# Two-layer diffusion backbone on one core: products by stream of 256 columns, operands moved by 64 bytes, the latent half first at the joins of stages

## The reference

```
z = modulate(rmsnorm(h), m0, m1);  h += 0.5*m2 * ((silu(z@Wg) * (z@Wu)) @ Wdown)   # 2 x 2816 columns, back to 1024
z = modulate(rmsnorm(h), m3, m4);  p = z @ W_in_mix                                # x, gelu input, u, v: 4 x 512
   RG-LRU: conv of x, sigmoid gates by head, forward and backward scan, * gelu
   spatial gate: u * (w_s @ layernorm(v) + b_s)
h += m5 * (concat(y_lru, y_sgu) @ W_out_mix)
z = modulate(rmsnorm(h), m6, m7);  h += 0.5*m8 * swiglu(z)
```

## Time and profile before

| | |
|---|---|
| median of 3 runs | 1624.05 us (1623.73 to 1624.52) |
| the profiled execution | 1623.73 us |
| its span | 1621.9 us |
| PE busy | 1572.3 us, 97%, 8,804 matmuls |
| PE weight loads | 1317.5 us, 81%, 8,804 |
| DVE busy | 1030.4 us, 64% |
| ACT busy | 633.2 us, 39% |
| POOL busy | 109.3 us, 7% |
| TensorE clock, mean | 0.99 of full |
| HBM read | 247.62 MB, 153 GB/s |

### The profile page before, as it was taken

One profiled execution on the slowest core, in us unless ns is written; L12 is line 12 of the kernel. 1 busy time (PEld: TensorE's weight loads), 2 busy tenths in 40 slices (PEclk: granted clock), 3 DMA queues, 4 the chain that ended last, 5 costly groups with the idle time before them and its releaser, 6 DMA issues.

```text
span 1621.9 us, 24555 instructions
## 1 busy us (share of the span) xinstructions
PE 1572.3 (97%) x8804; PEld 1317.5 (81%) x8804; DVE 1030.4 (64%) x1498; ACT 633.2 (39%) x841; POOL 109.3 (7%) x117
## 2 busy tenths in 40 slices
PE   5999999999999999999999999999999999789998
PEld 4788888888778787788888888888888877789997
DVE  6777778233777467787742368777753368856554
ACT  4322222222663364334422242222222248467752
POOL 0000000011200300000000110000001030110001
PEclk9999999999999999999999999999999999999999
DMA  9455555343322335555533325555533323445563
GB/s 379 148 182 189 183 188 187 130 156 129 92 78 73 110 112 179 188 183 186 186 124 101 114 91 183 188 186 186 189 125 109 103 78 117 142 149 193 191 208 117
DMA packets 89047, 249.43 MB, mean 154 GB/s; under 512 B 13472, under 2 KB 14624, under 8 KB 87840
## 3 DMA queue, kind: packets, MB, share of 16 engines
q1 hardware_dynamic: 88992, 248.71, 47.0%
HBM read 247.62 MB, written 1.05 MB: 153 GB/s over the span
## 4 chain that ended last, share of the span: by engine, by line
PE 88%; DVE 5%; issue 2%; DMA 2%; ACT 1%; POOL 1%; DVEq 0%; SPq 0%; POOLq 0%; ACTq 0%
PE bank L361 27%; PE bank L362 27%; PE bank L363 27%; DMA ada_raw<-ada_w 2%; PE bank L612 1%; DVE ada_acc L1030 1%; PE bank L381 1%; DVE w_lo L851 1%; PE bank L594 1%; PE bank L592 1%; PE bank L593 1%; DMA res<-x_t 0%; PE bank L465 0%; PE bank L407 0%; POOL tokr L1302 0%
## 5 line engine op out<-in xcount | busy, mean ns | idle before, releaser
L851 DVE TENSOR_TENSOR w_lo<-raw,w_hi 128x1024 fp32r<-128x1024 f32 x320 | 391.5, 1225 | 416.2 <-ACT w_hi L677 249.9
L361 PE MATMUL bank<-z_hi,w_hi 128*128 128x512 f32 (+1 forms) x1574 | 575.7, 366 | 8.3 <-DVE v_n L1160 2.7
L362 PE MATMUL bank<-z_lo,w_hi 128*128 128x512 f32 (+1 forms) x1574 | 567.6, 361 | 0.0
L363 PE MATMUL bank<-z_hi,w_lo 128*128 128x512 f32 (+1 forms) x1574 | 567.0, 360 | 0.0
L683 ACT ACTIVATE w_hi<-raw 128x1024 fp32r<-128x1024 f32 x176 | 186.5, 1060 | 428.2 <-PE bank L363 427.4
L361 PEld LDWEIGHTS bank<-z_hi,w_hi 128*128 128x128 f32 x1574 | 296.3, 188 | 63.0 <-issue 10.0
L363 PEld LDWEIGHTS bank<-z_hi,w_lo 128*128 128x128 f32 x1574 | 296.2, 188 | 46.0
L362 PEld LDWEIGHTS bank<-z_lo,w_hi 128*128 128x128 f32 x1574 | 296.4, 188 | 45.7 <-issue 1.9
L1030 DVE SCALAR_TENSOR_TENSOR ada_acc<-ada_raw,c_cols,ada_acc 128x512 f32<-128x512 f32 x420 | 288.9, 747 | 8.0 <-DMA ada_raw<-ada_w 6.7
L677 ACT ACTIVATE w_hi<-raw 128x1024 fp32r<-128x1024 f32 x136 | 143.9, 1059 | 350.8 <-PE bank L363 344.5
L361 PE MATMUL bank<-h_hi,w_hi 128*128 128x512 f32 (+1 forms) x704 | 254.2, 361 | 0.1
(11 more groups left out here) (136 smaller groups left out, 1069.4 us busy)
## 6 DMA issues: line engine op xcount, KB each, us to landing
raw<-weights SPq DMA_DIRECT2D x320, 512.0 KB, 3.3
ada_raw<-ada_w SPq DMA_DIRECT2D x240, 256.0 KB, 3.0
ada_head<-head_w SPq DMA_DIRECT2D x8, 1024.0 KB, 20.3
ada_z<-ada_w SPq DMA_DIRECT2D x4, 1024.0 KB, 5.8
res<-x_t SPq DMA_DIRECT2D x1, 2048.0 KB, 8.0
bd<-gate_w SPq DMA_DIRECT2D x4, 256.0 KB, 5.3
out<-res SPq DMA_DIRECT2D x4, 256.0 KB, 2.2
ws<-sgu_w SPq DMA_DIRECT2D x2, 256.0 KB, 5.6
```

The source lines that it names most:

```text
L361: pe.matmul(bank_ap, w_hi[:, r, c], rhs_hi, start=start, stop=False, skip_group_check=True)
L362: pe.matmul(bank_ap, w_hi[:, r, c], rhs_lo, start=False, stop=False, skip_group_check=True)
L363: return pe.matmul(bank_ap, w_lo[:, r, c], rhs_hi, start=False, stop=stop, skip_group_check=True)
L851: dve.tensor_tensor(w_lo[:, r, :], raw[:, r, :], w_hi[:, r, :].bitcast(F32), ALU.subtract).then_inc(lo_ready, 1)
```

## The change

Products are made by stream: each of the three matmuls of a product is issued for columns 0 to 255 and for 256 to 511, with the same weight block. `LAT0` goes, every operand starts at column 0, and `row_pad` moves from ahead of h to ahead of `raw`, `w_hi` and `w_lo`, which moves these and all up to h by 64 bytes, while z, h and y stay. At the joins with two streams (norms 1 to 4) the last row of a down stage (the last two rows of the out stage of layer 0) is computed for the latent stream first; the sums and the spread of the latent half stand amid the context products. The first slots (three in mix too) run all blocks of the latent half, then all of the context half; the context half's sums and spread stand behind blocks 1 and 4. The gap units of norm 1 move ahead of the last row. All of z_lo goes to VectorE. The mix stage shifts by one slot (`GATE_LAG` 3), the spatial gates get four banks, slot 12 waits for all eight copies, and all of `y_hi` is made at slot 15.

```diff
-GATE_LAG = 2
-SIDE = 2
-UP_SIDE = 3
+GATE_LAG = 3
+SIDE = 3
-MIX_HI_DVE = range(6, 10)
+MIX_HI_DVE = range(7, 11)
-LAT0 = 112
         z_lo = sb("z_lo", [P, KD, T], F32R)
+        sb("row_pad", [P, 16])
         raw = sb("raw", [P, RING, SLOT])
...
-        sb("row_pad", [P, 16])
...
-        x_bank = pa[0:2] + po
+        x_bank = pa[0:3] + po[1:2]
+        ss_bank, spread_bank = (p_misc, po[0]), (po[1], p_misc)
...
+        def split_rows(n):
+            return () if n == 0 or streams(dft(n)) == 1 else (6, 7) if n % 3 == 2 else (7,)
...
+        def tail_bank(d, s, n):
+            return po[d % 2] if s == 0 or d not in split_rows(n) else pa[3] if d == KD - 1 else p_ada
...
-            def product(bank_ap, blk, r, rhs_hi, rhs_lo, start, stop):
+            def product(bank, blk, r, x_hi, x_lo, k, ss, start, stop):
                 c = slice(blk * P, (blk + 1) * P)
-                pe.matmul(bank_ap, w_hi[:, r, c], rhs_hi, start=start, stop=False, skip_group_check=True)
-                pe.matmul(bank_ap, w_hi[:, r, c], rhs_lo, start=False, stop=False, skip_group_check=True)
-                return pe.matmul(bank_ap, w_lo[:, r, c], rhs_hi, start=False, stop=stop, skip_group_check=True)
+                for i, (w, x) in enumerate(((w_hi, x_hi), (w_hi, x_lo), (w_lo, x_hi))):
+                    for s in ss:
+                        m = pe.matmul(bank[:, COLS[s]], w[:, r, c], x[:, k, COLS[s]], start=start and i == 0 and s == ss[0],
+                                      stop=stop and i == 2, skip_group_check=True)
+                return m
...
+                for s in ss:
+                    for k in range(KD):
+                        c = slice(k * P, (k + 1) * P)
+                        pe.wait_ge(z_hi_ready, z_piece(n, k, s))
+                        for q, dst in enumerate(banks):
+                            pe.matmul(dst[:, COLS[s]], w_hi[:, q, c], z_hi[:, k, COLS[s]], start=(k == 0 and s == 0),
+                                      stop=False, skip_group_check=True)
+                            pe.matmul(dst[:, COLS[s]], w_lo[:, q, c], z_hi[:, k, COLS[s]], start=False,
+                                      stop=False, skip_group_check=True)
+                        pe.wait_ge(z_ready, z_piece(n, k, s))
...
+                        if len(ss) == 2 and s == 0:
+                            if k == 1:
+                                norm_sums(n, 1)
+                            if k == 4:
+                                norm_spread(n, 1)
...
+                def row_by_stream(d):
+                    q = 3 * d
+                    pe.wait_ge(lo_ready, at["slot"] + q + 3)
+                    pe.wait_ge(res_ready, HID0 - 1 + at["tile"] + d)
+                    for s in ss:
+                        for k in range(8):
+                            m = product(tail_bank(d, s, n), k, q % RING, h_hi, h_lo, k, (s,), k == 0, False)
+                    m.then_inc(slot_done, 1)
+                    for s in ss:
+                        for k in range(8, KF):
+                            m = product(tail_bank(d, s, n), k % 8, (q + k // 8) % RING, h_hi, h_lo, k, (s,), False, k == KF - 1)
+                            if s == 0 and k == KF - 1:
+                                m.then_inc(lat_done, 1)
+                            if s == 1 and k in (15, KF - 1):
+                                m.then_inc(slot_done, 1)
+                            if s == 1 and k == 12:
+                                norm_sums(n, 0)
+                            if s == 1 and k == 18:
+                                norm_spread(n, 0)
...
+                    if AT["norm", n]["gap"]:
+                        for k in range(KD):
+                            gap_unit(n, k)
+                    row_by_stream(KD - 1)
...
                     if q == 12:
                         pe.wait_ge(vn_ready, l + 1)
+                        pe.wait_ge(copy_ready, 8 * (l + 1))
...
-                        dst = (p_ada, p_misc)[g % 2]
+                        dst = (p_ada, p_misc, po[0], po[1])[g]
...
+                def rows_by_stream():
+                    pe.wait_ge(lo_ready, at["slot"] + KD)
+                    for s in ss:
+                        for d in split_rows(n):
+                            if s == 0:
+                                pe.wait_ge(res_ready, HID0 - 1 + at["tile"] + d)
+                            for k in range(KD):
+                                m = product(tail_bank(d, s, n), k, d % RING, y_hi, y_lo, k, (s,), k == 0, k == KD - 1)
+                                if k == KD - 1:
+                                    m.then_inc(slot_done if s else lat_done, 1)
+                                if s == 1 and d == 6 and k == 4:
+                                    norm_sums(n, 0)
+                                if s == 1 and d == 7 and k == 1:
+                                    norm_spread(n, 0)
                 pe.wait_ge(copy_ready, 8 * (l + 1))
+                pe.wait_ge(zz_ready, 4 * (l + 1))
...
# ScalarE, mix stage
-                    for k in {14: (0, 1), 15: range(2, KD)}.get(q, ()):
+                    for k in range(KD) if q == 15 else ():
# ScalarE, norm
+                for d in split_rows(n):
+                    square_half(d, n, 0)
+                act.wait_ge(slot_done, base - 1)
+                split_hi(base + 2, 2)
+                if len(split_rows(n)) == 2:
+                    square_half(6, n, 1)
+                z_high(0, 0)
+                z_high(1, 0)
+                square_half(7, n, 1)
+                for k in range(2, KD):
+                    z_high(k, 0)
...
# VectorE, norm
+                for i, d in enumerate(split_rows(n)):
+                    dve.wait_ge(lat_done, split_before(n) + i + 1)
+                    residual(n, d, 0, res_lat_ready)
...
+                if split_rows(n):
+                    split_lo(base + 2, 2)
...
+                for s in range(streams(w)):
+                    scaled(0, s)
+                    for k in range(KD):
+                        if k + 1 < KD:
+                            scaled(k + 1, s)
+                        z_low(k, s)
+                        if split_rows(n) and s == 0 and k == 0:
+                            dve.wait_ge(slot_done, base)
+                            residual(n, KD - 1, 1, res_ready)
+                        if split_rows(n) and s == 0 and k == 3:
+                            variance(1)
+                        if split_rows(n) and s == 1 and k == 2:
+                            split_lo(base + 3, 3)
# VectorE, mix stage
-                    if q in (6, 7):
-                        scans(l, q - 6)
+                    if q in (7, 8):
+                        scans(l, q - 7)
...
+                    if q == 15:
                         y_low(l, 0, wl)
+                        spatial_gate(l, 3, wl)
                         y_low(l, 1, wl)
```

More of the change, by code:

```diff
@@ L506, in first_slots @@
[L506 to L511 removed]
+                for s in ss:
[8 more added lines that the diff above has]
+                        pe.wait_ge(z_ready, z_piece(n, k, s))
+                        for q, dst in enumerate(banks):
+                            m = pe.matmul(dst[:, COLS[s]], w_hi[:, q, c], z_lo[:, k, COLS[s]], start=False,
+                                          stop=(k == KD - 1 and s == ss[-1]), skip_group_check=True)
+                            if k == KD - 1 and s == ss[-1]:
+                                m.then_inc(slot_done, 1)
[4 more added lines that the diff above has]
+                                norm_spread(n, 1)
@@ L547, in down_stage @@
                 at = AT[l, "down", f]
[L548 to L564 removed]
+                n = 3 * l + 2 * f + 1
@@ new lines, in down_stage, with row @@
+                ss = range(streams(dft(n - 1)))
+                def row(d, dd):
+                    for part, n_blk in enumerate((8, 8, 6)):
+                        q = 3 * dd + part
+                        pe.wait_ge(lo_ready, at["slot"] + 1 + (d - dd) * 3 + q)
+                        if part == 0:
+                            pe.wait_ge(res_ready, HID0 - 1 + at["tile"] + d)
+                        for b in range(n_blk):
+                            k = 8 * part + b
+                            if dd == 0 and k in (0, KF - 2, KF - 1):
+                                pe.wait_ge(hid_lo_ready, HID_LO0 + at["ffn"] * KF + max(k + 1, KF - 2))
+                            m = product(po[dd % 2], b, q % RING, h_hi, h_lo, k, ss, k == 0, k == KF - 1)
+                        m.then_inc(slot_done, 1)
@@ L566, in in_stage @@
+                with pe.Fori(0, KD // 4 - (len(ss) == 2)) as i:
+                    for dd in range(4):
+                        row(i * 4 + dd, dd)
+                if len(ss) == 2:
+                    for d in range(4, KD - 1):
+                        row(d, d)
+                    if AT["norm", n]["gap"]:
+                        for k in range(KD):
+                            gap_unit(n, k)
+                    row_by_stream(KD - 1)
```

(22 more changed lines are left out.)

363 lines of the change are left out of this document (140 added, 223 removed).

## The result

The changed kernel takes 1643.84 us (median of 4 runs, 1640.48 to 1653.52) beside 1624.28 for the kernel before in the same session (1623.73 to 1624.76): ratio 1.013, 95% interval 1.0087 to 1.0173. Forecast were 1618.9 and a range up to 1627. The profiled execution took 1644.79, its span is 1642.8. The four runs of after lie 13 us apart, those of before 1 us.

A forecast was written before the change was run, and what follows sets the result against it. TensorE's chain of waits, 88% of the page's chain, was taken as the bound. From 1623.73 us, joins gave -11.7 and mix stages +1.5, +2.45 and +2.9, making 1618.9; the range was 1612 to 1627.

The forecast's parts named there:

- (a): Products of both streams: splitting each 512-column matmul into two of 256 costs 0; bounds 0 and 6.7 ns per half.
- rival B: Placement fails: one or both halves of a product run at 120 ns; 1653 or 1687 us, chance 0.12.
- the v slots: Slots streaming weights at +64 over z, 96 matmuls on layer 0's path: between -0.4 and +1.3 us, taken as 0.
- Rival C: Every matmul has a fixed price, paid once more per pair: 0.8 ns together, 4.1 us, 1623.0 us; chance 0.05.
- (b): Joins 3 and 4, last row by stream: 4.0 us left lost (3.1 to 5.5), gaining 2.7 and 4.2.
- (c): Join 2, mix to up, last two rows by stream: 4.3 us left lost (3.9 to 5.6), gaining 2.4.
- (d): Join 1, down to mix, with eight gap units now on the path: 8.1 us left (7.2 to 9.6), gaining 2.4.
- joins 1 to 4: Stage changes down to mix, mix to up, down to up, down to mix (layer 1): 32.1 us lost before the change.
- the 0.50 clock: Granted clock of 1.2 GHz for 3.4 us after idle time in joins 2 to 4; should go with the idle time.
- (e): Layer 0's mix stage, shifted by one slot: new waits of +1.5 us ahead of slot 12 and +2.45 at y.
- (f): Layer 1's mix stage, where VectorE sets the time: +2.9 us (0 to +5).
- Rival D: Mix stages take all gains back, with (f) at +5 and joins at upper bounds: 1621 to 1627 us, chance 0.18.

The follow-up runs named there:

- e3: The changed kernel with z, h, y and the weights all moved by another 448 bytes modulo 512, their distance kept: 1644.78 us, ratio 1.0101.
- e8: The changed kernel with moving rows and weights 112 bytes apart modulo 256 in every product: 1628.25 us, ratio to the kernel before 0.9984.
- e9: The changed kernel with w_lo moved by 128 bytes against w_hi: 1627.29 us, ratio to the kernel before 0.9974.
- m1: Kernel without the model's computation, matmul stretches at varied distance and form: 256 columns at distance 192 took 113.3 ns in 16 of 32 stretches, otherwise 117.8.
- m2: Second kernel without the computation, distances in 16-byte steps: at 112 all six stretches of 256 columns settled at 113.3 ns.
- e4: The kernel before with only the 64-byte move (LAT0 = 0, row_pad ahead of raw), products still 512 columns: 1656.91 us, ratio 1.0175.
- e6: The kernel before with each 512-column product matmul issued as two of 256, placement unchanged: 1695.04 us, ratio 1.0402.
- e10: The kernel before with LAT0 = 28, so one-stream stages read from column 28 instead of 112: 1625.35 us, ratio 0.9973.
- e11: e9 with VectorE's last two scan pairs of the mix stage put ahead of its waits for slots 12 and 13: 1626.07 us.
- e12: e11 with y products 0 to 3 taken behind slots 12 and 13, their high parts and low parts 0, 1 at slot 14: 1623.21 us, ratio 0.997.

## Why the prediction was wrong

**(a), the step that failed.** It put the pairs at zero: "Modulo 512 bytes all three are the same number ... I expect 113 ns for both halves." The arithmetic of the addresses was right, and e3 (another place, the same distance, the same mixture) with e8 and e9 (another distance, no mixture) shows that the distance is what counts. What failed is the conclusion from it: a stretch at this distance at 113 ns was taken as the price of the distance, where it was one of two. At distance 192 a 256-column matmul goes at 113.3 or 117.8 ns, taken at a restart and then kept (m1, m2, and the 262 stretches). 796 matmuls in one stretch are one draw, not 796. The term put at 0 measured +17.4 us.

The bounds of (a) were right in kind, 0 to 6.7 ns per half, and the truth (4.5 ns on 37% of the gaps) lay inside. The range didn't hold them: 1653 stood in rival B alone, at 0.12. That rival had the kind, "the placement fails", and even its doubt ("I know from one offset pair"), but one fixed price and not two paces, and that price too high because it took the 120 ns of distance 0. That the rows said nothing of 512 columns at -64 was noted and priced at the v slots only; e4 shows the move with 512 columns to cost more (31 us) than with the pairs, and e6 that the pairs without the move would cost 70 us.

**Rival C.** A fixed price per matmul would have to show wherever there are pairs. The stretches at 113.3 in after, e8 and e9 show none: 796 or 797 in 90 us, as in the earlier trace rows, twice the 399 of 512 columns (e10). The rule of the Trainium skill ("TensorE: Matmul & The Clock Gate", "Back-to-back issue gap", 2.5 ns per matmul), which the section itself calls the gap of an isolated matmul, is not borne out on these rows.

**(b), (c), (d), the joins: right.** Left over were forecast 8.1, 4.3, 4.0 and 4.0 us (joins 1 to 4), measured 7.5, 4.0, 3.7 and 3.8; the gain is 12.6 us for 11.7, and the 0.50 clock is gone from the joins, as forecast. The first stall was larger (953.75 to 954.94 in join 3, about 1.1 us for 0.2) and the later ones smaller.

**(e): right.** The wait at slot 12 came (494.26 to 495.93 between starts, "ACT gl", 1.4 us idle for 1.5) and the one at y (521.27 to 523.82 between starts, 2.3 us idle for 2.45). The stage lost 4.4 us for 3.95.

**(f): right in kind, short in size.** Layer 1's mix stage lost 4.9 us more for 2.9, at the upper bound of 5, and the wait at y was 6.6 us for "7". The sum had no term for the wait ahead of slot 12 (v_n), which grew from 2.7 to 5.8 us; with the other wait (5.7 us on y_sgu before, 6.6 after) TensorE stands 4.0 us longer than before, and no experiment touched the v_n part. e11 shows that part of the wait at y was VectorE's order. That what stays is VectorE's work itself is argued from e12's timeline, which has no pause left.

**What was costed at nothing** and wasn't: the long stages and the out stages, +6.7 us over the whole span between these two profiles. The out stage's +1.1 is the half clock behind layer 0's wait at y (1.5 us there), which the prediction charged in layer 1 alone; some of the rest is scatter between executions, as the half clock in e8 shows, and what remains is open. With it joins and mix stages come to +3.4 us, not -4.9. So even without the pace the change would not have been faster: e8 and e9, at 1627 to 1628, are 2 to 3 us over e10. Rival D had that outcome (1621 to 1627), but only in part its reasons: (f) was at +5 as it said, the joins were not at their upper bounds but under the forecast. e12 takes back a part of the mix stages and comes level with the kernel before.

## What to carry to other kernels

Before a matmul's form or its operands' addresses are changed, look at the pace in several stretches that start apart: one long stretch shows one of the steady paces that an address distance allows, and says nothing of the others. When PE is busy at full clock and the kernel still gets slower, count starts per stretch and compare two stretches of the same code; then measure the form at every distance in a kernel of its own, which took two runs here and found the two placements that take the slow pace away. A reorder that lets the next stage start three slots at once moves everything behind it on VectorE's queue: price that queue to its end before counting the gain at the join.

## What the runs showed of the hardware

- The pace of float32r matmuls goes by the distance of weights and moving rows modulo 256 bytes. 512 columns: 226.7 ns at 0, 233.3 at 192. 256 columns: 120.0 at 0, 118.7 at 128, 113.3 or 117.8 at 64 and 192, 113.3 in all stretches at 112. The best distance for 512 columns, 0, is among the slowest for 256.
- Where two paces exist, the one taken lasts over hundreds of matmuls: 767 in 90 us in one stage, 797 in its twin, and no change inside any of 262 stretches.
- Loading the weights again for each half of a product costs nothing by itself: at 113.3 ns a pair takes what the wide form takes, 226.7.
- What makes the two paces inside the chip, and what picks one at a start, is open; the runs show at which distances there are two.
